# Differential attention: values as the stationary operand, two steps' probabilities moving, a head's norm from a column of ones and rows in DRAM, and its steps four ticks sooner

## What is computed

```python
def differential_attention(q, k, v, lam):      # q,k: (B,S,H,2,Dh); v: (B,S,H,2Dh)
    def one_block(qblk):                       # 128 queries
        s = einsum('bihce,bjhce->bhcij', qblk, k) * (Dh ** -0.5)
        p = softmax(s, axis=-1)
        a = p[:, :, 0] - lam * p[:, :, 1]
        return einsum('bhij,bjhe->bihe', a, v)
...
yd = differential_attention(qd, kd, vd, lam)   # 8 heads of 128 columns
yd = rms_norm(yd, diff_subln) * (1.0 - lambda_init)
yd = yd.reshape(B, S, DIFF_V_WIDTH) * silu(zd)
pb = yd @ w_proj_b
```

## Time and profile before

| | |
|---|---|
| time before, median of three runs | 801.05 us (800.49 to 1100.22) |
| the profiled execution: its own time | 801.21 us |
| its span, first to last instruction | 799.1 us |
| outside the span | 2.1 us |
| PE busy | 778.6 us, 97% of the span |
| POOL, DVE, ACT busy | 452.4, 420.2 and 359.9 us |
| mean granted clock of TensorE | 0.992 |

### The profile page before, as it was taken

The page is one execution under the profiler, slowest core; times in us unless marked ns, Lnnn a source line. Parts: engine busy times, 40 slices in busy tenths (PEclk is TensorE's granted clock), DMA queues, the critical chain, the costliest instruction groups (busy, mean ns, idle before and its releaser), DMA issues.

```text
span 799.1 us, 12588 instructions
## 1 busy us (share of the span) xinstructions
PE 778.6 (97%) x4590; PEld 656.9 (82%) x4590; DVE 420.2 (53%) x692; ACT 359.9 (45%) x777; POOL 452.4 (57%) x577
## 2 busy tenths in 40 slices
PE   4999999999999999999999999999999999999997
PEld 3787898888888888898797888888787878878997
DVE  4766664635455443344675576487557445324432
ACT  5555535545444444343464555455556333314311
POOL 7854545446656654369663696596454287837200
PEclk9799999999999999999999999999999999999999
DMA  9955323233343432352431433242212145615431
GB/s 317 348 168 155 86 84 104 81 98 115 107 119 105 121 107 80 107 151 81 140 97 54 121 105 121 78 123 76 82 34 74 35 151 213 208 53 177 139 106 53
DMA packets 87075, 95.38 MB, mean 119 GB/s; under 512 B 9405, under 2 KB 78310, under 8 KB 87014
## 3 DMA queue, kind: packets, MB, share of 16 engines
q1 hardware_dynamic: 86944, 94.56, 38.3%
q10 hardware_dynamic: 70, 0.02, 0.0%
HBM read 78.53 MB, written 5.54 MB: 105 GB/s over the span
## 4 chain that ended last, share of the span: by engine, by line
PE 90%; issue 3%; POOL 3%; DVE 1%; DMA 1%; ACT 1%; SPq 0%; DVEq 0%; POOLq 0%; ACTq 0%
PE proj L1747 64%; PE sums L1670 4%; PE proj L1867 4%; PE score L1586 4%; PE turned L1638 3%; PE score L1620 3%; PE proj L1796 2%; PE sums L1672 2%; POOL w_lo L819 1%; PE score L1608 1%; DMA x_in<-in_x 1%; PE score L1796 1%; PE turned L1680 0%; PE turned L1694 0%; POOL merged L796 0%
## 5 line engine op out<-in xcount | busy, mean ns | idle before, releaser
L819 POOL TENSOR_TENSOR w_lo<-raw,w_hi 128x256 fp32r<-128x256 f32 x376 | 299.9, 829 | 212.7 <-ACT w_hi L932 212.7
L1747 PE MATMUL proj<-h_hi,w_hi 128*128 128x512 f32 x560 | 229.4, 410 | 0.1
L1747 PE MATMUL proj<-h_hi,w_lo 128*128 128x512 f32 x560 | 219.3, 392 | 0.0
L1747 PE MATMUL proj<-h_lo,w_hi 128*128 128x512 f32 x560 | 218.7, 391 | 0.0
L1747 PEld LDWEIGHTS proj<-h_hi,w_hi 128*128 128x128 f32 x560 | 105.2, 188 | 30.4 <-issue 9.6
L1747 PEld LDWEIGHTS proj<-h_hi,w_lo 128*128 128x128 f32 x560 | 105.1, 188 | 23.2
L1747 PEld LDWEIGHTS proj<-h_lo,w_hi 128*128 128x128 f32 x560 | 105.5, 188 | 19.1 <-issue 0.5
L932 ACT ACTIVATE w_hi<-raw 128x1024 fp32r<-128x1024 f32 x96 | 100.4, 1054 | 15.7 <-PE proj L1747 11.2
L1380 DVE TENSOR_TENSOR at_lo<-turned,at_hi 128x512 fp32r<-128x512 f32 x64 | 44.1, 689 | 80.6 <-ACT at_hi L1070 80.0
L848 POOL TENSOR_TENSOR rope_x<-rope_x,cos_t 128x512 f32<-128x512 f32 x36 | 53.4, 1484 | 51.6 <-DMA rope_s<-rope_x 51.6
L1670 PE MATMUL sums<-v,at_hi 128*128 128x128 f32 (+1 forms) x256 | 60.8, 307 | 0.0
(11 more groups left out here) (291 smaller groups left out, 1479.7 us busy)
## 6 DMA issues: line engine op xcount, KB each, us to landing
raw<-in_w_in SPq DMA_DIRECT2D x85, 512.0 KB, 3.6
rope_s<-rope_x SPq DMA_DIRECT2D x144, 64.0 KB, 2.0
ada<-in_w_ada SPq DMA_DIRECT2D x24, 256.0 KB, 7.1
raw<-in_w_proj_b SPq DMA_DIRECT2D x8, 512.0 KB, 3.4
zd<-in_w_ada SPq DMA_DIRECT2D x8, 512.0 KB, 4.6
raw<-in_w_out SPq DMA_DIRECT2D x8, 512.0 KB, 4.2
rows_in<-window_rows SPq DMA_DIRECT2D x4, 792.0 KB, 5.8
window_rows<-rows_out SPq DMA_DIRECT2D x4, 528.0 KB, 5.0
```

What stands on the lines that cost most here:

```text
L819: nc.gpsimd.tensor_tensor(lo[:, k, :], raw_place(n)[:, k, :], hi.bitcast(F32)[:, k, :], ALU.subtract).then_inc(w_lo_done, 1)
L1747: ins = mm(dst, left, right, start=k == 0 and n == 0, stop=k == nk - 1 and n == 2, skip_group_check=tile.b == 2)
```

## The change

1. **Steps.** The steps of a differential stage begin at `T0[n+1] - 4`, while the stage's own zd block is still being projected, and end four ticks sooner.
2. **Products with the values.** `pv` of parts 0 and 2 does nothing. In parts 1 and 3 it makes both parts' products: the values are stationary (`v_hi`, `v_hi`, `v_lo`), and two slots of `at_hi` or `at_lo` move together as 2 x 128 columns; 12 products of 256 columns for two parts. `at_hi` and `at_lo` get a third slot. What lands in `sums` has the head's columns on the partitions and the 512 queries along the free dimension, so neither `copy_sums` nor `head_turn` is needed.
3. **Norm.** VectorE multiplies `sums` by `zd` at once (`head_gate`). ScalarE squares the 128x512 `sums` and cuts the squares in two (tick p+1), VectorE subtracts (`head_lo`), TensorE multiplies a column of 1/128 with both halves (`head_share`, tick p+2: two products of 512 columns with one output row), ScalarE copies that row out and issues a DMA to `share_rows` (p+2), then a DMA that reads it back as 128x4 (p+3); GpSimd makes eight small operations on it (p+4); ScalarE issues a DMA of the 128x4 result to `rstd_rows` (p+5) and one that reads it as a row of 512 into all 128 partitions (p+6); VectorE multiplies (`head_norm`, p+7). ScalarE waits for each DMA before it issues the next.

```diff
-        begin = t0[n + 1] + (0 if n else 2) + (g in (1, 2))
+        begin = t0[n + 1] - 4 if g == 3 else t0[n + 1] + (0 if n else 2) + (g in (1, 2))
...
+    for s in steps:
+        n = (0, 2, 1, 2)[s.part] if s.group == 3 else s.s % 2
+        at_slot[s.s], at_before[s.s] = n, user.get(n)
+        user[n] = s.s + (s.group == 3 and s.part % 2 == 0)
...
-    y_at = by_tick(diff_ends, lambda s: free_turn(s.pv + 4))
+    y_at = by_tick(diff_ends, lambda s: free_turn(s.pv + 2))
+    cols_at = by_tick(diff_ends, lambda s: s.pv + 3)
+    norm_at = by_tick(diff_ends, lambda s: s.pv + 4)
+    store_at = by_tick(diff_ends, lambda s: s.pv + 5)
+    load_at = by_tick(diff_ends, lambda s: s.pv + 6)
+    final_at = by_tick(diff_ends, lambda s: s.pv + 7)
...
             def head_squares(s):
                 n = diff_ends.index(s)
-                act.wait_ge(peak_done, n + 1)
-                for qt in range(NT):
-                    ins = nc.scalar.activation(junk[:], head_sums[:, s.hd % 2, qt * P:(qt + 1) * P], ACT.Square,
-                                               scale=ystat[:, 2, qt:qt + 1], accum_out=ystat[:, 3, qt:qt + 1])
-                    ins.then_inc(squares_done, 1)
-                    act.wait_ge(squares_done, NT * n + qt + 1)
+                act.wait_ge(head_read, n + 1)
+                act.wait_ge(head_done, n)
+                nc.scalar.activation(square, sums[:], ACT.Square, scale=st[:, 58:59]).then_inc(squares_done, 1)
+                act.wait_ge(squares_done, 2 * n + 1)
+                nc.scalar.activation(square_hi[:], square, ACT.Copy).then_inc(squares_done, 1)
+
+            def norm_rows(s):
...
+                nc.scalar.activation(gate_row[0:1, S:2 * S], turned[0:1, :], ACT.Copy).then_inc(t_read, 1)
+                act.wait_ge(t_read, turned_no["y", s.hd] + 1)
+                act.dma_start(share_rows[n:n + 1, :], gate_row[0:1, S:2 * S]).then_inc(row_stored, 16)
+
+            def norm_cols(s):
+                n = diff_ends.index(s)
+                act.wait_ge(row_stored, 16 * (n + 1))
+                act.dma_start(ystat[:, 3, :], share_rows[n].rearrange("(c p) -> p c", p=P), allow_slow_non_contiguous=True).then_inc(row_landed, 16)
+
+            def norm_store(s):
+                n = diff_ends.index(s)
+                act.wait_ge(pow_done, n + 1)
+                act.dma_start(rstd_rows[n].rearrange("(c p) -> p c", p=P), ystat[:, 1, :], allow_slow_non_contiguous=True).then_inc(rstd_stored, 16)
+
+            def norm_load(s):
+                n = diff_ends.index(s)
+                act.wait_ge(rstd_stored, 16 * (n + 1))
+                act.dma_start(square, rstd_rows[n].partition_broadcast(P)).then_inc(rstd_landed, 16)
...
+            def head_norm(s):
                 n = diff_ends.index(s)
-                dve.wait_ge(t_filled, turned_no["y", s.hd] + 1)
-                dve.wait_ge(z_done, Z_DONE[n])
-                stt(out=zd[:, n, :], in0=turned[:], scalar=cols[:, 41:42], in1=zd[:, n, :],
-                    op0=ALU.mult, op1=ALU.mult).then_inc(t_read, 1)
+                dve.wait_ge(rstd_landed, 16 * (n + 1))
+                dve.wait_ge(head_read, n + 1)
+                tt_(zd[:, n, :], zd[:, n, :], square, ALU.mult).then_inc(head_done, 1)
...
             def pv(s):
+                if s.group == 3 and s.part % 2 == 0:
+                    return
...
+                    for kt in range(NT):
+                        keys_ = slice(kt * P, (kt + 1) * P)
+                        v_hi, v_lo = (v[:, kt, w, s.head * P:(s.head + 1) * P] for w in range(2))
+                        hi, lo = (at[:, pair:3:2 - pair, keys_] for at in (at_hi, at_lo))
+                        mm(to, v_hi, hi, start=kt == 0, stop=False, skip_group_check=True)
+                        mm(to, v_hi, lo, start=False, stop=False, skip_group_check=True)
+                        ins = mm(to, v_lo, hi, start=False, stop=kt == NT - 1, skip_group_check=True)
+                    ins.then_inc(pv_done, 2)
+                    return
...
-            def head_turn(s):
+            def head_share(s):
...
+                pe.wait_ge(square_lo_done, n + 1)
+                mm(turned[0:1, :], share[:, 0:1], square_hi[:], start=True, stop=False)
+                mm(turned[0:1, :], share[:, 0:1], square_lo[:], start=False, stop=True).then_inc(t_filled, 1)
```

More of the change, by code:

```diff
@@ L82, in __init__ @@
         self.rows = slice(HD * (head % 2), HD * (head % 2) + HD)
-        self.copies = self.group or head % 2
+        self.copies = self.group in (1, 2) or (self.group == 0 and head % 2)
 def plan():
@@ L315, in build @@
         block2_lo = [spare("block2_lo0")]
+        scope = ExitStack()
+        square_lo, square_hi = (sb(f"square_{w}", [P, S], F32R, scope) for w in ("lo", "hi"))
+        scope.close()
         gate_row = sb("gate_row", [P, D])
@@ L611, in den0, with at_place, at_free @@
             return dens[:, s.hd % 2, 0, s.part:s.part + 1]
+        square = gate_row[:, 0:S]
+        def at_place(s):
+            n = at_slot[s.s]
+            return at_hi[:, n, :], at_lo[:, n, :]
+        def at_free(engine, s):
+            if at_before[s.s] is not None:
+                engine.wait_ge(pv_done, at_before[s.s] + 1)
         def yd_at(i, k):
@@ L1116, in _ @@
                     vt_hi(tile)
+                for s in y_at(t):
+                    norm_rows(s)
+                for s in cols_at(t):
+                    norm_cols(s)
+                for s in store_at(t):
+                    norm_store(s)
+                for s in load_at(t):
+                    norm_load(s)
                 for tile in rope_add_at(t):
@@ L1510, in _ @@
                         out_lo(half)
+                for s in head_lo_at(t):
+                    head_lo(s)
                 for s in trans_at(t):
@@ L1641, in pv @@
             def pv(s):
+                if s.group == 3 and s.part % 2 == 0:
+                    return
                 pe.wait_ge(t_read, turned_no["step", s.s] + 1)
-                if s.head == 0 and s.part == 0:
+                if s.head == 0 and s.part == (1 if s.group == 3 else 0):
                     if s.stage in v_of:
@@ L1647, in pv @@
                         pe.wait_ge(t_read, turned_no["vt", vt_of[s.stage]] + 1)
+                v = stage_mem(s.stage)["v"]
+                if s.group == 3:
+                    pair = s.part // 2
+                    if pair == 0:
+                        n = diff_ends.index(next(e for e in diff_ends if e.hd == s.hd))
+                        pe.wait_ge(sums_copied, COPIED_BEFORE[s.s])
+                        pe.wait_ge(squares_done, 2 * n)
+                        pe.wait_ge(head_read, n)
+                    to = sums[:, 2 * P * pair:2 * P * (pair + 1)]
+                    for kt in range(NT):
[7 more added lines that the diff above has]
+                    return
@@ new lines, in pv @@
+                width, col0 = HD, s.head * HD
+                n_q = 2 if s.group == 0 else 4
+                products_ = []
+                for i in range(n_q):
+                    qt = 2 * s.part + i if s.group == 0 else i
+                    keys = [(qt - 1) % NT, qt] if s.group == 0 else [qt]
+                    for m, kt in enumerate(keys):
+                        to = qt * P if s.group else i * P + (s.head % 2) * HD
+                        products_.append(((i * len(keys) + m) * P, kt, to, m == 0, m == len(keys) - 1))
```

154 lines of the change are left out of this document (71 added, 83 removed).

## The result

867.57 us (865.77 to 868.95, four runs), against 801.15 for the kernel before: ratio 1.0822, 95% interval 1.0806 to 1.0839. The kernel is 66 us slower, and my range ended at 809. One of the four executions of the kernel before took 1100.22 us; the ratio is of fast runs alone.

The account below looks back on a forecast made before the run. TensorE, busy for 97% of the span, was taken to bound the kernel. 801.2 - 6.0 (products) + 0 (turn) + 4.4 (hole) + 1.7 (clock) + 0.3 (later starts) + 0 (norm) = 801.6 us, range 796.8 to 809.

Parts of the forecast that it names:

- Part 5: Norm's chain of DMAs and GpSimd operations: covered by projections mid-kernel, thin cover at the last head; 0 us, from -1.0 to +3.
- Part 4: Starts of the three later stages: scores wait for k_lo, 0.1 us each, 0.3 us in all; bound 0 to 3 each.
- the norm's DMAs hold ScalarE and VectorE: Rival, chance 0.17: single-number DMAs take 5.8 us, delaying three stage starts and the last head; 815.6 us, 808 at half.
- threshold of 3.5 us: Length of a single-number DMA past which the slow-DMA rival decides, using up the slack ahead of k_hi.
- The seven ticks, 28 us of room: Mid-kernel, last pv to head_norm: seven ticks of about 4 us against some 20 us of norm work, covered by projections.
- Part 1: Products with the values: 12 products of 256 columns, 0.12 us each, per pair of steps; 6.0 us saved.
- Part 2: Head's turn replaced by two products with the column of ones: 0.46 us a head either way, so nothing.
- Part 3: Stage 6 starting four ticks sooner: TensorE waits 4.4 us for the last key tile; bounds 0 to 7.
- The clock behind it: After the stage 6 hole, TensorE's clock falls to half for 3.4 us, costing 1.7 us; bounds 0 to 5.
- clock kept: Rival, chance 0.24: the wait at stage 6 comes but the clock stays at 2.4 GHz; 799.9 us.
- No hole: Rival, chance 0.05: stage 6's key tile is ready because the swap's DMAs land sooner; 795.5 us.
- dear products: Rival, chance 0.04: new value products, two slots moving, cost 0.17 us each and are no cheaper; 811.2 us.

Follow-up runs that it names:

- good layout: Changed kernel with the store to rstd_rows written as 128 runs of 16 bytes, read back through a strided view: 803.68 us, ratio 1.0022.
- without the norm: Changed kernel without a head's four DMAs and GpSimd's eight operations, zd multiplied by the squares' low half instead: 800.61 us, ratio 0.999.

## Why the prediction was wrong

- **The step that failed: Part 5, "four DMAs of about 3.3 us at most".** I priced a store of 512 single numbers by `mix_in`, a load of 768 pieces of 32 bytes. It was the nearest row by count and the wrong one by kind: it reads, and its pieces are 32 bytes long. The store took 9.5 us. The reading one took 2.2 us and the broadcast 3.8 when undisturbed, near what I gave them. The first store, of one row, has no landing time in the trace, but its wait let the next DMA be issued 1.8 to 2.6 us after it. The same figure carried Part 4's bound of 0 to 3 us for each stage start: TensorE waited 4.7, 6.9 and 5.3 us there.
- **The rival "the norm's DMAs hold ScalarE and VectorE"** was the truth, at 0.17, with 815.6 us at its full price, because its bound was 5.8 us (`rows_in`). With 9.5 its own working gives some 6 us at three stage starts and twice at the end, about 832. Three things were missing in it: the other head of each stage, whose `head_norm` holds the turn (21 us of gaps); that the store holds up the transfers of others (+18 us by itself); and the clock (some 17 us). Its threshold of 3.5 us lies between the two that were measured, 1.4 us with none of it left and 9.5 us with all of it; where between them it turns was not tried.
- **The seven ticks, 28 us of room, did not help.** Each DMA has one tick of its own, of about 4 us, since the wait stands in ScalarE's order one tick behind the issue. Room in the sum of a chain does not help where each link is waited for in order.
- **Part 1 held.** 6.0 us were forecast. From the first product of tick `T0[8]` to that of `T0[9]`, eight steps, the kernel before takes 65.3 us (438.16 to 503.50), the one with the good layout 64.0 (445.45 to 509.44), the stage after that 65.8 and 64.3: 1.4 us a stage, 5.7 for four. Part 2 is within that and at nothing.
- **Part 3 held.** 4.4 us forecast at the same place with the same cause; 3.4 us after the change, 3.8 in the good layout, 4.4 without the norm. The clock behind it: forecast 3.4 us at half and 1.7 lost; 3.4 us at half and 1.5 lost in the good layout, not at all after the change, 6.8 us without the norm. There is one profile of each kernel, and the granted clock differs between executions of one kernel (above), so the rival "clock kept" was true of the profiled execution of the kernel after and says nothing of the others. "No hole" and "dear products" are out. That the kernel after waited 3.4 us and not 4.4 was no part of the forecast; the swap came 1 us sooner.
- **Part 4 held with the good layout**: no wait for `k_lo` at the three other stages. After the change these waits are 17 us.
- **The sum.** With the good layout 803.7 us were measured and 801.6 forecast; the waits at 600 and 604 us (0.5 and 1.1 us), behind the block of `ya_split_tick`, stood in no part of it. Nor did 0.6 us more ahead of the last b block and 0.7 us for `w_lo` at 672. These 2.9 us are about the difference; that it is met so nearly is in part luck, since each part is good to some tenths of a microsecond.

## What to carry to other kernels

Where a change adds a DMA of a form that the trace does not show, take its form apart (read or write, bytes in a run, what lies beside it) before it is priced by a row, and if one end of the bound is open, the range has to be open too. A store of single numbers side by side is to be laid out in runs of 16 bytes, and the permutation paid where it is read. And a wait that an engine makes in order is priced against the tick between issue and wait, for every time it stands there, with the engine's whole queue behind it.

## What the runs showed of the hardware

A store of 4-byte numbers side by side takes 8.1 us for 128 of them and 9.1 to 12.3 us for 512, whose packets are over within 0.4 us (421.2 to 421.6). With a gap of 4, 12, 28, 60 or 508 bytes between them it takes 2.0 to 3.8 us. With runs of 16 bytes it takes mostly 1.4 to 2.7, and up to 5.6 us in the kernel with three of them one behind the other. While a store side by side is out, a broadcast load behind it takes 7 to 12 us in place of 3 to 5, and loads of weights on SyncE's queue 10.4 in place of 3.6. And the time at half clock costs less than its half: 51 us at 1.2 GHz cost some 17 us, since TensorE stood for a good part of them anyway (busy for 6.4 of 11 us in the stretch from 476 us).
